# The last stage of a hybrid decoder layer step: combining and normalising five token tiles on one, and on three, engines

## The reference

```python
h = layer_norm(ALPHA * h + mix, ln1_g, ln1_b)
h = layer_norm(ALPHA * h + hier_moe(h, ...), ln2_g, ln2_b)

def layer_norm(x, g, b):
    mu = mean(x); var = mean(square(x - mu))
    return (x - mu) * rsqrt(var + LN_EPS) * g + b

# hier_moe: top-1 group, top-2 experts inside it
y = sum over the two chosen experts of prob[k] * expert_k(x)
```

## Time and profile before

| | us |
|---|---|
| three runs | 960.98, 962.42, 966.94 |
| median | 962.42 |
| the profiled execution | 960.92 |
| its span in the profile | 959.1 |

### The profile page before, as it was taken

The page is one execution under the profiler, slowest core; times in us unless marked ns, Lnnn a source line. Parts: engine busy times, 40 slices in busy tenths (PEclk is TensorE's granted clock), DMA queues, the critical chain, the costliest instruction groups (busy, mean ns, idle before and its releaser), DMA issues.

```text
span 959.1 us, 12358 instructions
## 1 busy us (share of the span) xinstructions
PE 828.2 (86%) x4741; PEld 591.0 (62%) x4741; DVE 474.1 (49%) x1074; ACT 263.4 (27%) x650; POOL 199.1 (21%) x172
## 2 busy tenths in 40 slices
PE   5999898999989896999999899989899987976910
PEld 5997798989878794788888644587333332322300
DVE  5998365757576668885136324372131101010158
ACT  4221443434354247574412111111011101010100
POOL 2664424242103361110000000004211111011000
PEclk9999899999998797999999999979999999896965
DMA  8320211111043122573622193276999999999152
GB/s 312 88 90 18 82 45 44 45 45 45 1 187 114 52 97 91 217 245 131 243 110 88 47 429 138 67 287 222 351 422 424 423 425 419 424 426 374 51 190 87
DMA packets 34474, 182.15 MB, mean 190 GB/s; under 512 B 10996, under 2 KB 11652, under 8 KB 23857
## 3 DMA queue, kind: packets, MB, share of 16 engines
q1 hardware_dynamic: 25488, 159.24, 42.6%
q0 software_dynamic: 7744, 17.86, 5.3%
q10 hardware_dynamic: 1184, 4.26, 1.1%
HBM read 169.03 MB, written 20.77 MB: 198 GB/s over the span
## 4 chain that ended last, share of the span: by engine, by line
PE 59%; DVE 19%; DMA 14%; issue 3%; POOL 1%; ACT 1%; SPq 1%; POOLq 0%; DVEq 0%; ACTq 0%
PE bank L584 10%; PE bank L585 9%; PE bank L586 9%; DMA y_f<-in_w_gu 8%; PE bank L1017 7%; PE bank L577 6%; DVE r_f L1479 6%; PE bank L1026 4%; DMA x_f<-scr_id 2%; PE bank L768 2%; PE bank L674 1%; PE bank L800 1%; DMA small_f<-scr_h,x_f 1%; PE bank L708 1%; PE bank L799 1%
## 5 line engine op out<-in xcount | busy, mean ns | idle before, releaser
L1017 PE MATMUL bank<-x_f,r_f 128*64 128x512 f32 x272 | 126.9, 622 | 9.8 <-DMA y_f<-in_w_gu 9.0
L584 PE MATMUL bank<-r_r,w_r 128*128 128x268 f32 x416 | 126.0, 303 | 10.7 <-DVE w_r L1456 10.1
L585 PE MATMUL bank<-y_r,w_r 128*128 128x268 f32 x416 | 122.7, 295 | 0.0
L586 PE MATMUL bank<-r_r,w_r 128*128 128x268 f32 x416 | 122.7, 295 | 0.0
L585 PE MATMUL bank<-w_r,r_r 128*128 128x512 f32 x240 | 96.3, 401 | 0.0
L584 PEld LDWEIGHTS bank<-r_r,w_r 128*128 128x128 f32 x416 | 82.3, 198 | 15.6 <-DVE w_r L1456 10.1
L584 PE MATMUL bank<-x_r,r_r 128*128 128x512 f32 x200 | 81.8, 409 | 3.9 <-DVE w_r L1763 3.8
L585 PEld LDWEIGHTS bank<-y_r,w_r 128*128 128x128 f32 x416 | 82.4, 198 | 0.0
L586 PEld LDWEIGHTS bank<-r_r,w_r 128*128 128x128 f32 x416 | 82.2, 198 | 0.0
L586 PE MATMUL bank<-x_r,w_r 128*128 128x512 f32 x200 | 80.4, 402 | 0.0
L1017 PEld LDWEIGHTS bank<-x_f,r_f 128*64 128x64 f32 x272 | 38.3, 143 | 63.0 <-issue 63.0
(11 more groups left out here) (371 smaller groups left out, 1552.2 us busy)
## 6 DMA issues: line engine op xcount, KB each, us to landing
x_f<-in_w_gu SPq DMA_DIRECT2D x17, 2048.0 KB, 29.6
w_f<-in_w_d SPq DMA_DIRECT2D x22, 1024.0 KB, 29.7
y_f<-in_w_gu SPq DMA_DIRECT2D x10, 2048.0 KB, 28.0
w_f<-in_w_f SPq DMA_DIRECT2D x26, 512.0 KB, 3.7
w_f<-in_w_gu SPq DMA_DIRECT2D x6, 2048.0 KB, 23.0
x_f<-in_w_d SPq DMA_DIRECT2D x11, 1024.0 KB, 33.5
w_f<-in_w_t SPq DMA_DIRECT2D x5, 2048.0 KB, 8.1
y_f<-in_state POOLq DMA_DIRECT2D x8, 512.0 KB, 4.7
```

Source lines behind the costliest of these rows:

```text
L584: pe.matmul(out, ah, bh, start=start, stop=False)
L585: pe.matmul(out, ah, bl, start=False, stop=False)
L586: return pe.matmul(out, al, bh, start=False, stop=stop)
L1017: ins = pe.matmul(out[half, :], XT[:, k, half], wgu[s][:, k, :], start=(k == 0), stop=(k == KC - 1))
```

## The change

The stage is divided over three engines, and the tiles are taken in another order: 1, 2, 0, 3 (the tuple `TAIL`), and 4 at the end.

- Tile 0's combining leaves VectorE: ScalarE multiplies both gathered tiles of 8 rows in place by their factors, and GpSimd adds them to the hidden state, one after the other (`pool_final`, new).
- For the tiles in `TAIL` the shift leaves VectorE and becomes two instructions: ScalarE multiplies the tile by the reciprocal (after a new semaphore `rs_dv` from VectorE), and GpSimd adds the bias (after `rs_ac` from ScalarE). GpSimd then releases the store (`o_pl`).
- VectorE keeps the combines of tiles 1 to 4, the statistics, centring and reciprocal of all five, and the whole of tile 4's shift. A tile's reciprocal now follows its own centring directly. From the third tile on, the statistics wait until ScalarE has used the reciprocal of two tiles before (`rs_ac`), as that buffer of `lmv` is used again.
- SyncE stores in the new order. `act_root` takes the number of rows as an argument; its first-norm calls are the same as before.

```diff
+TAIL = (1, 2, 0, 3)
...
-            for t in range(NT):
-                sp.wait_ge(S["o_dv2"], t + 1)
+            for t in (*TAIL, NT - 1):
+                if t in TAIL:
+                    sp.wait_ge(S["o_pl"], TAIL.index(t) + 1)
+                else:
+                    sp.wait_ge(S["o_dv2"], 1)
...
         def act_final(act):
 
-            for t in range(NT):
-                act_root(act, NT + t + 1)
+            act.wait_ge(S["gt0"], 32)
+            for k in range(2):
+                ins = act.activation(G[k][0:NSAMP, 0, :], G[k][0:NSAMP, 0, :], ACT.Copy, scale=prob[0:NSAMP, k, 0:1])
+            ins.then_inc(S["gs_ac"], 1)
+            for i, t in enumerate(TAIL):
+                r = tile_rows(t)
+                act_root(act, NT + i + 1, r)
+                act.wait_ge(S["rs_dv"], i + 1)
+                act.activation(h1[0:r, t, :], h1[0:r, t, :], ACT.Copy, scale=lmv[(NT + i) % 2][0:r, 3:4])\
+                   .then_inc(S["rs_ac"], 1)
+            act_root(act, 2 * NT, P)
...
-            def gathered(t):
+            def combined(t):
                 r = tile_rows(t)
                 h = h1[0:r, t, :]
                 v.wait_ge(S[f"gt{t}"], 32)
-                link(v.scalar_tensor_tensor(h, G[0][0:r, t, :], prob[0:r, 0, t:t + 1], h, ALU.mult, ALU.add))
-                link(v.scalar_tensor_tensor(h, G[1][0:r, t, :], prob[0:r, 1, t:t + 1], h, ALU.mult, ALU.add))
-                norm_stats(v, h, r, NT + t + 1)
-
-            def finished(t):
+                for k in range(2):
+                    link(v.scalar_tensor_tensor(h, G[k][0:r, t, :], prob[0:r, k, t:t + 1], h, ALU.mult, ALU.add))
+
+            def centred(i, t):
                 r = tile_rows(t)
-                norm_apply(v, h1[0:r, t, :], r, NT + t + 1, lnr[0:r, 3, :], lnr[0:r, 4, :]).then_inc(S["o_dv2"], 1)
-
-            gathered(0)
-            for t in range(1, NT):
-                gathered(t)
-                finished(t - 1)
-            finished(NT - 1)
+                h = h1[0:r, t, :]
+                if i >= 2:
+                    v.wait_ge(S["rs_ac"], i - 1)
+                norm_stats(v, h, r, NT + i + 1)
+                return v.scalar_tensor_tensor(h, h, lmv[(NT + i) % 2][0:r, 0:1], lnr[0:r, 3, :], ALU.subtract, ALU.mult)
+
+            def rooted(i, t):
+                r, mv = tile_rows(t), lmv[(NT + i) % 2]
+                v.wait_ge(S["lv_ac"], NT + i + 1)
+                return v.reciprocal(mv[0:r, 3:4], mv[0:r, 2:3])
+
+            for i, t in enumerate(TAIL):
+                if t:
+                    combined(t)
+                else:
+                    v.wait_ge(S["gs_pl"], 2)
+                link(centred(i, t))
+                rooted(i, t).then_inc(S["rs_dv"], 1)
+            t = NT - 1
+            combined(t)
+            link(centred(t, t))
+            link(rooted(t, t))
+            v.scalar_tensor_tensor(h1[:, t, :], h1[:, t, :], lmv[(NT + t) % 2][:, 3:4], lnr[:, 4, :], ALU.mult, ALU.add)\
+             .then_inc(S["o_dv2"], 1)
...
+        def pool_final(p):
+
+            h = h1[0:NSAMP, 0, :]
+            p.wait_ge(S["gs_ac"], 1)
+            for k in range(2):
+                p.tensor_tensor(h, h, G[k][0:NSAMP, 0, :], ALU.add).then_inc(S["gs_pl"], 1)
+                p.wait_ge(S["gs_pl"], k + 1)
+            p.wait_ge(S["ln2_in"], 16)
+            for i, t in enumerate(TAIL):
+                r = tile_rows(t)
+                p.wait_ge(S["rs_ac"], i + 1)
+                p.tensor_tensor(h1[0:r, t, :], h1[0:r, t, :], lnr[0:r, 4, :], ALU.add).then_inc(S["o_pl"], 1)
```

More of the change, by code:

```diff
@@ L334, in build @@
                      "htr_mm hte_dv dn_mm y_ev ex_mm ex_ac ex_dv ex_in yw_out0 yw_out1 "
-                     "gt0 gt1 gt2 gt3 gt4 o_dv2 o_out "
+                     "gt0 gt1 gt2 gt3 gt4 gs_ac gs_pl rs_dv rs_ac o_pl o_dv2 o_out "
                      "small_out kv_out out_d dve_chain act_chain").split():
@@ L1345, in act_squares, with act_root @@
             act_link[0](ins)
-        def act_root(act, n):
-            r, mv = tile_rows((n - 1) % NT), lmv[(n - 1) % 2]
+        def act_root(act, n, r):
+            mv = lmv[(n - 1) % 2]
             act.wait_ge(S["lv_dv"], n)
@@ L1382, in act_mix @@
                 merged(t)
-            act_root(act, 1)
+            act_root(act, 1, tile_rows(0))
             merged(3)
-            act_root(act, 2)
+            act_root(act, 2, tile_rows(1))
             merged(4)
-            act_root(act, 3)
+            act_root(act, 3, tile_rows(2))
             first(0)
-            act_root(act, 4)
+            act_root(act, 4, tile_rows(3))
             first(1)
             first(2)
-            act_root(act, 5)
+            act_root(act, 5, tile_rows(4))
             first(3)
@@ L2297, in _ @@
             pool_experts(p)
+            pool_final(p)
 def constants():
```

## The result

The changed kernel takes 967.14 us (median of 8 runs, 966.07 to 971.09) against 962.17 us (8 runs) for the kernel before, a ratio of 1.005 with an interval of 1.0033 to 1.0066: slower by half a per cent. That is within one per cent, as forecast, on the forecast's side and inside its range of 958.0 to 970.5, but 2.8 us above its 964.3 and 0.6 us above the 962 to 966.5 that it gave for scatter alone.

The account below looks back on a forecast made before the run. VectorE alone was taken to bound the last stage. Unhindered -4.13 us, beginning +2.88, three shifts beside combines +1.20 and the sample tile +1.95 gave +1.90, put on the 962.42 median: 964.3 us, range 958.0 to 970.5.

Parts of the forecast that it names:

- Unhindered sum, -4.13 us: Last stage: without engines hindering each other, VectorE needs 27.00 us and ends at 951.94, 4.13 us before 956.07.
- Beginning, 2.88 lost: Tile 1: GpSimd's two additions hold VectorE's combines; reciprocal ends at 933.55 instead of 930.67, 2.88 us lost.
- The sample tile, 1.95 lost: Tile 2's shift on GpSimd holds the sample tile's centring; reciprocal at 4.95 instead of 3.00 us, 1.95 lost.
- Statistics run beside GpSimd: Last stage: statistics, having one input, are not held by GpSimd's additions; a block costs 6.05 us, otherwise 7.68.
- the second rival: Blocks with combines: GpSimd holds statistics too, blocks of 7.68 us, 4.9 us more, 969.2 us; first two rivals together 0.30.
- Three blocks of 6.05: Tiles 2, 3 and 4 beside GpSimd shifts: second combine just ahead, centring waits; 0.40 us lost each, 1.20 in all.
- The sum: Last stage: -4.13 + 2.88 + 1.20 + 1.95 = +1.90 us; VectorE ends at 957.97, median 964.3 us.
- Start: Last stage: VectorE begins with tile 1, whose first combine starts at 924.94, 3.76 us later than before.
- The first rival: Combine blocks: GpSimd comes before the second combine three times, blocks of 7.71 us, 969.3 us; first two rivals together 0.30.
- No hindrance: Last stage: combines and centrings run beside GpSimd's additions, so all of 4.13 us stays, 958.3 us; chance 0.13.

Follow-up runs that it names:

- e4_first_shift_prompt: Changed kernel with a one-column fill on GpSimd ahead of the shift loop, taking over two of the first shift's three waits; 970.12 us, ratio 1.01.
- e6_sample_first: Changed kernel with the sample tile first and combined by VectorE, GpSimd doing only the four shifts, unordered; 964.8 us, ratio 1.0013.
- e3_gpsimd_later: Changed kernel with GpSimd filling one column and waiting for it ahead of each of the four shifts; 964.06 us, ratio 1.0017.
- e10_first_later: Changed kernel with the sample tile first and combined by VectorE, plus a one-column GpSimd fill and wait before each shift; 959.74 us, ratio 0.9967.

## Why the prediction was right, and where it was off

- *Unhindered sum, -4.13 us.* Right: 26.98 us against 27.00 once GpSimd is out. ScalarE's scaling took 1.15 us (1.13 forecast), and no root held a reciprocal.
- *Beginning, 2.88 lost.* From the first combine to the reciprocal's end 935.35 - 926.82 = 8.53 us, 2.80 more than the 5.73 of the earlier trace rows. The combines took 2.13 and 3.25, forecast 2.10 and 3.36. A held instruction ended sooner after its release than the forecast's 1.16 us: in tile 2 (939.53 + 1.61) - (936.70 + 3.35) = 1.09, and 1.08 or 1.09 for every other held combine or centring of 1024 columns. That is the 0.07 of tile 2's block and most of the sample's 0.09.
- *The sample tile, 1.95 lost.* Its block took 4.86 against 4.95, its centring 3.15 against the 3.2 named.
- *Statistics run beside GpSimd.* Right: they take 0.69 and 0.68 us while the addition works, so the second rival falls. The Trainium skill, page "SBUF — State Buffer", section "SBUF: two separate sides", had it so, and the runs with PSUM agree: one input in SBUF, own length.
- *Three blocks of 6.05.* The step that failed: "The second starts at 1.22, just ahead, and ends at 2.50." Both times were right (1.22 and 1.26 after the reciprocal's end at 946.19), and what followed from them was wrong: a recorded start 0.04 us ahead did not give VectorE the port. The forecast had this from the pair at 62.51 in the earlier trace rows, where VectorE kept such a lead; the last section says how that pair differs. One block took 5.98, two took 7.82: 2 x 1.77 = 3.54 us more than forecast. By the same section of the Trainium skill whichever of the two starts first gets the port; by the recorded starts the measurement differs here, and it decides. That the one block came out as forecast is luck: its shift had two more waits, and came 0.13 us behind and not 0.04.
- *The sum.* Start -0.19 (924.75 against 924.94 on the clock of before), beginning -0.08, tile 2 -0.07, the sample -0.09, tiles 3 and 4 +3.54: 3.11 us, and 1.90 + 3.11 = 5.01 as measured. The first rival was the truth for two blocks of three. Its reason, a ScalarE scaling nearer to 1.05, was not: GpSimd's start was recorded when I had said.
- *No hindrance.* This rival falls at the first combine, 2.13 us beside the addition. Its time, 958.3, is about what the run without GpSimd has, 959.3.

The forecast lay on the right side because its terms came from rows of the same operations and of the same exclusion; its range held only because it reached to the rivals: of the first one's three long blocks two came.

## What to carry to other kernels

Work that left VectorE for GpSimd was no gain by its own length here, since most of VectorE's long instructions have two inputs in SBUF: each GpSimd addition is to be priced as time taken from VectorE, less only what lies beside instructions with one input or beside none. Then look at where the requests meet. A delay of 0.16 us at GpSimd, an order behind the second combine, or an operand kept in PSUM each took back more than half of the loss, 2.7 to 3.6 us of 5.0. None of them alone made a gain; with VectorE also combining the sample tile first, the delay, PSUM, or PSUM together with the order gained 0.3 to 0.4% on the kernel before. In a profile such waiting counts as busy time, so compare the mean of a group with the same form elsewhere before believing that an engine is full.

## What the runs showed of the hardware

Recorded starts within 0.05 us of each other don't tell which of the two engines goes first. In eight pairs of combines (two in after, three each in e4_first_shift_prompt and e6_sample_first) GpSimd's start was recorded 0.04 or 0.05 us after that of the second combine, and GpSimd went first. In nine (the short blocks of after and e6_sample_first, three of e3_gpsimd_later, four of e10_first_later) it came 0.11 to 0.29 us after, and GpSimd waited.

In the earlier trace rows, at 62.51 and 62.55, VectorE kept a lead of 0.04, and it did so in all nine pairs of this kind in the kernel before. There too VectorE waits for its own instruction before (at 62.51 L1479 for L1484, by the semaphore `rope_dv`), which ends at 61.69 + 0.72 = 62.41:

```profile
61.69 0.72 DVE L1484 TENSOR_TENSOR x_f<-r_f 128x536 f32<-128x536 f32 x1
```

So the start of L1479 is recorded 0.10 us after that end, and that of a second combine only 0.03 or 0.04. Counted from the end of VectorE's instruction before, GpSimd started 0.07 or 0.08 us later in the eight pairs in which it went first, and 0.14 us or more later in all the others. This count sorts every one of these pairs, with the boundary between 0.08 and 0.14 us, where the recorded start of VectorE does not. It is read from the traces afterwards: no run moved that end by itself, and why the two kinds of instruction differ is open. Instructions that don't wait for the one before them are outside it.
